# A hybrid decoder step on one core: eight weight slots in place of six, the cache copies at other tiles, weights laid out in long runs

## The chip, the cores and the metric

The kernel runs on one core of one Trainium2 chip. The metric is the device time of one execution in microseconds (us). Before the change, three runs gave a median of 1416.43 us (1415.73 to 1416.78).

## The reference, cut to what matters

One layer of a decoder, all in float32, for 256 prompt tokens and 8 sample tokens together (T = 264 columns, D = 1024):

```
h = rmsnorm(x); z = h @ w_in                      # 68 tiles of 128 columns: q, k, v, lru x, gates
b_lru = (rglru(conv(xr)) * gelu(gr)) @ w_br_lru    # recurrent branch
b_att = attention(q, k, v, caches) @ w_br_att      # 3 groups of dilated windows, 4 heads each
x = x + (sigmoid(g_lru)*b_lru + sigmoid(g_att)*b_att) @ w_out
x = x + moe(rmsnorm(x))                            # 32 experts, top 4, clamped SwiGLU
x = x + sigmoid(rmsnorm(x) @ w_ple_gate) * (p @ w_ple)
kv_g*_sample = cache shifted by one row, new k, v appended   # a copy of nearly the whole cache
```

Each expert has a 1024 x 2048 matrix (gate, up) and a 1024 x 1024 matrix (down): 12 MB, read once. The three sample caches (8 samples, windows of 128, 512 and 1024 rows of 4 KB) are copied to outputs with all rows one place down.

## The kernel before, in words

Five engines run their own instruction lists and meet at semaphores. SP issues nearly all loads, ACT (beside its activations) issues the cache copies, POOL issues small stores and the experts' biases. TensorE (PE) is the engine with the most work.

**Front.** The projection z runs in 68 tiles (`z_tile(n)`, L522 for its matmuls). Its weights come in 17 pieces of 2 MB (`win(piece)`, L393), four tiles each. Pieces 0 to 9 rotate through four ring slots, later ones through two; SP waits for `z_done` before it refills a slot: piece 9 when 24 tiles are done, piece 10 at 36, piece 11 at 40, piece 14 at 52. PE needs piece p at tile 4p. Between the tiles PE does other work in a written order: query and key norms after tile 25, the recurrent gates (L568) after tiles 41 to 44, transposes to token order (L554) after 45 to 50, prompt attention (L582, L594, L602) after 51 to 60, sample attention after 61 to 66. The transposes need `roped`, which VectorE (DVE) gives with L1255 after a small DMA of POOL has landed.

ACT evacuates each tile from PSUM (`evac`, L974) and between evacuations issues copies: `shift(g, b)` (L980) copies the cache of group g and sample b inside HBM, without its first row: 448 KB for group 0, 1984 KB for group 1, 4032 KB for group 2. The copies for groups 0 and 1 go out every fourth tile. Those of group 2 go out three together after tile 23, then after tiles 35, 43 and 51, and the last two (samples 6 and 7) when the first tile of the w_out product (L726) is done. The few rows that remain follow in `shift_rest`.

After the z tiles come the products with w_br_lru (L691), w_br_att (L701) and w_out (L726), whose halves SP loads (`half`, L433) with four runs of 4 KB for each partition; then the router and the PLE product p @ w_ple (L757).

**Experts.** The 32 experts run one after the other, each in six pieces of 2 MB: gate 0, gate 1, up 0, up 1, down 0, down 1. The ring has six slots, so piece s of expert e goes into the slot that piece s of expert e-1 leaves:

```python
for s in range(6):
    sp.wait_ge(used[s], n)
    sp.dma_start(slot(s), weights(e, s)).then_inc(full[s], 16)
```

SP issues the loads at L478. PE multiplies a piece with L789 (16 matmuls) and spreads the previous expert's rows to the tokens in between (L829). Expert 0's six pieces are loaded while the products ahead of the experts run. Experts 2 to 30 are one loop of PE, `pe.Fori(2, E - 1)`, with one expert in a pass. Code for the case that more than 64 tokens choose one expert (`further`) stands behind it and is jumped over when it isn't needed.

**Tail.** When gate 1 of expert 31 is done (`g1_mm`), SP loads the 4 MB of w_ple_gate into two slots. PE then does the PLE gate product (L937, L947), which waits for both halves, and the result is stored in four DMAs (L492). At the end SP waits for all stores and cache copies.

Of the kernel before, what the change touches and what calls it, by code (L numbers as in the profile page):

```python
# [14 lines left out]
P = 128  # L15
D = 1024
KT = D // P
NP, NS = 256, 8
T = NP + NS
# [6 lines left out]
DIL = (1, 4, 16)  # L26
SKEYS = tuple(w // d for w, d in zip(WB, DIL))
E = 32
# [5 lines left out]
CH = 512  # L34
# [27 lines left out]
class Signals:  # L62


    def __init__(self, sem):
# [76 lines left out]
        self.lru_x = sem("lru_x")  # L142
# [44 lines left out]
        self.bdn_in = sem("bdn_in")  # L187
# [16 lines left out]
        self.w5 = sem("w5")  # L204
        self.g0_mm = sem("g0_mm")
# [38 lines left out]
def build(nc, a):  # L244

    with ExitStack() as ctx:
        def sb(name, shape, dt=F32):
            return ctx.enter_context(nc.sbuf_tensor(name, shape, dt))
# [12 lines left out]
        hT = sb("hT", [P, KT, T])  # L261
        xc = sb("xc", [P, KT, T])
        lt = sb("lt", [P, KT, T])
# [28 lines left out]
        lt_flat = lt[:, :, :].rearrange("p k t -> p (k t)")  # L292
# [20 lines left out]
        wpl, pT = zb([P, 2, D]), zb([P, 2, T])  # L313
        wr = zb([P, KT, E])
# [16 lines left out]
        rparts = zb([P, T])  # L331
# [5 lines left out]
        wpg = [ring[:, SLOT[s], :].rearrange("p (k n) -> p k n", k=4) for s in (0, 1)]  # L337
# [6 lines left out]
        def further(eng, count, block_of, first, last, before=None, after=None):  # L344


            def chunk(c):
                if before is not None:
                    before(c)
                with eng.Fori(0, E) as e:  # L350
                    block_of(e, e + c * E)
# [32 lines left out]
        def _(sp):  # L384
# [42 lines left out]
            def cached_v(g, p0=0):  # L427
                n = SKEYS[g]
                src = a[f"cache{g}"].rearrange("b (k r) n -> k b r n", r=DIL[g])[:, :, 0, CH:2 * CH]
                sp.dma_start(vts[g][p0:p0 + n, :, :], src).then_inc(S.v_in, 16)  # L430
# [6 lines left out]
            cached_v(2, 64)  # L437
# [11 lines left out]
            sp.dma_start(wr[:, :, :], a["w_router"].rearrange("(k p) n -> p k n", p=P)).then_inc(S.wr_in, 16)  # L449
            sp.dma_start(wpl, a["w_ple"].rearrange("(k p) n -> p k n", p=P)).then_inc(S.wpl_in, 16)  # L450
            sp.dma_start(pT, a["pT"]).then_inc(S.wpl_in, 16)
            sp.dma_start(bdn, a["b_down"]).then_inc(S.bdn_in, 16)


            def weights(e, s):

                return a["wmoe"][e][s]

            def slot(s):
                return ring[:, SLOT[s], :]  # L460

            full = (S.w0, S.w1, S.w2, S.w3, S.w4, S.w5)
            used = (S.g0_mm, S.g1_mm, S.u0_mm, S.u1_mm, S.d0_mm, S.d1_mm)
            sp.dma_start(slot(0), weights(0, 0)).then_inc(S.w0, 16)
            sp.wait_ge(S.bl_mm, KT)
            sp.dma_start(slot(1), weights(0, 1)).then_inc(S.w1, 16)
            sp.dma_start(slot(2), weights(0, 2)).then_inc(S.w2, 16)
            sp.wait_ge(S.ba_mm, KT)
            sp.dma_start(slot(3), weights(0, 3)).then_inc(S.w3, 16)
            sp.wait_ge(S.wo_mm, KT)  # L470
            sp.dma_start(slot(4), weights(0, 4)).then_inc(S.w4, 16)
            sp.dma_start(slot(5), weights(0, 5)).then_inc(S.w5, 16)

            def load(e, n):

                for s in range(6):
                    sp.wait_ge(used[s], n)
                    sp.dma_start(slot(s), weights(e, s)).then_inc(full[s], 16)  # L478

            load(1, 1)  # L480
            count = load_most(sp)
            with sp.Fori(2, E) as e:
                load(e, e)
            further(sp, count, load, first=lambda: sp.wait_ge(S.d1_mm, E), last=lambda: sp.wait_ge(S.yb_zero, 1),
                    after=lambda n: sp.wait_ge(S.d1_mm, n))

            sp.wait_ge(S.g1_mm, E)
# [12 lines left out]
        def _(pe):  # L500
# [132 lines left out]
            def sample_attend():  # L633
                pe.wait_ge(S.st_ev, 3)
                pe.wait_ge(S.sb_ev, 1)
                pe.wait_ge(S.v_in, 64)
# [108 lines left out]
            pe.wait_ge(S.wpl_in, 32)  # L745
# [37 lines left out]
            def half_product(bank, src, slot):  # L783

                w = ring[:, SLOT[slot], :].rearrange("p (k n) -> p k n", k=4)
# [55 lines left out]
            def block_(n, following=True, alone=False):  # L841


# [6 lines left out]
                pe.wait_ge(S.w0, 16 * (n + 1))  # L850
                pe.wait_ge(S.xT_ok, n + 1)
                half_product(0, xgT, 0).then_inc(S.g0_mm, 1)
# [4 lines left out]
                pe.wait_ge(S.w1, 16 * (n + 1))  # L857
                half_product(0, xgT, 1).then_inc(S.g1_mm, 1)
                between(1)
                pe.wait_ge(S.w2, 16 * (n + 1))  # L860
                half_product(1, xgT, 2).then_inc(S.u0_mm, 1)
                between(2)
                pe.wait_ge(S.w3, 16 * (n + 1))
                half_product(1, xgT, 3).then_inc(S.u1_mm, 1)
# [11 lines left out]
                pe.wait_ge(S.w4, 16 * (n + 1))  # L876
                pe.wait_ge(S.hT_ok, n + 1)
                half_product(4, hmT, 4).then_inc(S.d0_mm, 1)
                pe.wait_ge(S.w5, 16 * (n + 1))
                half_product(4, hmT, 5).then_inc(S.d1_mm, 1)  # L880
# [22 lines left out]
            pe.wait_ge(S.bdn_in, 16)  # L903
            block_(0)
            block_(1)
# [5 lines left out]
            def apart(e, n):  # L911
                rows(n)
                rows_T(n)
                block_(n, following=False, alone=True)
                spread_all(n)

            further(pe, count, apart, first=lambda: spread_all(E - 1), last=lambda: pe.wait_ge(S.yb_zero, 1),
                    after=lambda n: pe.wait_ge(S.added, 4 * n + 4))
# [34 lines left out]
        def _(act):  # L953
# [69 lines left out]
            for n in range(24, NZ):  # L1023
# [7 lines left out]
                if n in (35, 43, 51):  # L1031
                    shift(2, n // 8 - 1)
# [54 lines left out]
            act.wait_ge(S.wo_mm, 1)  # L1087
            for b in range(6, NS):
                shift(2, b)
# [71 lines left out]

            root(3, rstd[:, :], PS[:, 0, 0:T], 1.0 / D).then_inc(S.rms_ok, 1)
# [6 lines left out]
        def _(v):  # L1169
# [92 lines left out]
            TT(X, X, xc[:, :, :], ALU.mult).then_inc(S.lru_x, 1)  # L1262
# [3 lines left out]
            v.wait_ge(S.lru_x, 1)  # L1266
# [358 lines left out]
def layout(i):  # L1625
# [5 lines left out]
    def cols(v):  # L1631
# [3 lines left out]

    order = [4, 5, 6, 7, 8, 9, 0, 1, 10, 11, 12, 2, 3, 13, 14, 15, 16]
# [10 lines left out]
        w_router=i["w_router"][0], b_router=np.ascontiguousarray(np.tile(i["b_router"], (P, 1))), w_br_lru=i["w_br_lru"][0], w_br_att=i["w_br_att"][0],  # L1647
        w_out=i["w_out"][0], w_ple_gate=i["w_ple_gate"][0],
        w_ple=i["w_ple"][0])
    for g in range(NG):  # L1650
        c = i[f"cache_kv_g{g}"][0]
        out[f"cache{g}"] = c.reshape(NS, WB[g], 2 * CH)
        out[f"kt{g}"] = np.ascontiguousarray(c[:, ::DIL[g], 0].transpose(3, 0, 2, 1)).reshape(P, -1)
# [54 lines left out]
```

## Time and profile before

| | |
|---|---|
| median of 3 runs | 1416.43 us |
| the profiled execution's own time | 1418.05 us |
| span of that execution | 1416.4 us |
| PE busy | 1350.0 us, 95% |
| DVE, ACT, POOL busy | 399.8, 182.4, 35.6 us |
| DMA moved | 531.41 MB, mean 375 GB/s |
| chain that ended last, by engine | PE 59%, DMA 39% |

The span runs from the first to the last instruction of the program. A number with L is a line of the kernel. A duration behind a DMA goes from its issue to its landing. "SPq" and "ACTq" are the instruction queues of SP and ACT, in which they wait and issue DMAs. q1 is the DMA queue that SP fills, q10 that of ACT, q0 that of POOL, q8 brings instructions.

### The profile page before, as it was taken

Reading aid. Unit: us, or ns where it says so; the run is one execution under the profiler, and the core shown is the slowest. Engines: PE = TensorE matmul, PEld = TensorE weight load, DVE = VectorE, ACT = ScalarE, POOL = GpSimd, SP = SyncE. Lnnn points to the kernel's source line nnn. Section 1 sums busy time; section 2 is a strip of 40 time slices with the busy share of each in tenths; the row PEclk is TensorE's granted clock in tenths of the full one; section 3 lists DMA queues with packets and bytes.
Section 4 is the critical chain, followed back from the end, with each engine's and each line's share of the span. In section 5 each row is a group of like instructions: output and inputs, shape, how many; then the busy total and the mean of one; then the engine's idle time right before and its main releaser. Section 6 shows DMA issues by size and latency. Waiting matters only on the chain.

```text
span 1416.4 us, 17044 instructions
## 1 busy us (share of the span) xinstructions
PE 1350.0 (95%) x7000; PEld 676.8 (48%) x7000; DVE 399.8 (28%) x636; ACT 182.4 (13%) x340; POOL 35.6 (3%) x62
## 2 busy tenths in 40 slices
PE   7999599899999999999999999999999999999988
PEld 6887488798874333333333333333333333333337
DVE  4106547320233222222222122221222212222134
ACT  1111034322003100010001000010000100000101
POOL 0001003000000000000000000000000000000000
PEclk9999899999999999999999999999999999999999
DMA  9889997958986999999999999999999999999980
GB/s 385 312 345 326 304 353 259 294 137 328 376 308 242 400 422 429 428 428 428 428 428 428 428 428 428 427 429 427 428 428 427 430 427 429 426 429 428 428 344 31
DMA packets 44886, 531.41 MB, mean 375 GB/s; under 512 B 6973, under 2 KB 7373, under 8 KB 16533
## 3 DMA queue, kind: packets, MB, share of 16 engines
q1 hardware_dynamic: 40784, 471.47, 80.9%
q10 hardware_dynamic: 1685, 54.43, 10.6%
q0 software_dynamic: 2384, 5.03, 1.2%
q8 instruction: 25, 0.41, 0.1%
q14 instruction: 8, 0.07, 0.0%
HBM read 526.15 MB, written 58.38 MB: 413 GB/s over the span
## 4 chain that ended last, share of the span: by engine, by line
PE 59%; DMA 39%; ACT 1%; DVE 0%; issue 0%; SPq 0%; DVEq 0%
DMA ring<-in_wmoe 33%; PE PS L789 25%; PE PS L522 16%; DMA ring<-in_win 5%; PE PS L829 2%; PE PS L726 2%; PE PS L691 2%; PE PS L803 2%; DMA ring<-in_w_ple_gate 2%; PE PS L937 1%; PE PS L947 1%; PE PS L701 1%; PE PS L568 1%; PE PS L815 1%; PE PS L795 1%; ACT Zb L1124 1%
## 5 line engine op out<-in xcount | busy, mean ns | idle before, releaser
L789 PE MATMUL PS<-ring,Zb 128*64 128x512 f32 x3072 | 687.6, 596 | 20.2 <-DMA ring<-in_wmoe 19.2
L789 PEld LDWEIGHTS PS<-ring,Zb 128*64 128x64 f32 x3072 | 209.4, 137 | 421.7 <-issue 378.7
L522 PE MATMUL PS<-hT,ring 128*128 128x264 f32 x1024 | 237.9, 392 | 21.8 <-DMA ring<-in_win 21.8
L522 PEld LDWEIGHTS PS<-hT,ring 128*128 128x128 f32 x1024 | 195.4, 193 | 58.5 <-DMA ring<-in_win 22.4
L1451 DVE TENSOR_TENSOR xc<-xc,PS 128x528 f32<-128x528 f32 x128 | 89.7, 701 | 171.8 <-PE PS L829 159.5
L1479 DVE COPY Zb<-PS 128x512 f32<-128x512 f32 x32 | 22.1, 692 | 326.7 <-PE PS L789 326.7
L829 PE MATMUL PS<-Zb 64*128 64x264 f32 x496 | 88.7, 435 | 0.0
L829 PEld LDWEIGHTS PS<-Zb 64*128 64x128 f32 x496 | 37.3, 184 | 100.6 <-issue 100.6
L1132 ACT ACTIVATE Zb<-Zb 128x512 f32<-128x512 f32 x32 | 20.2, 630 | 470.2 <-DVE Zb L1461 470.2
L1124 ACT ACTIVATE Zb<-PS 128x512 f32<-128x512 f32 x32 | 19.1, 597 | 358.0 <-PE PS L817 358.0
L803 PE MATMUL PS<-Zb 128*64 128x512 f32 x256 | 63.5, 617 | 0.0
L974 ACT ACTIVATE Zb<-PS 128x264 f32<-128x264 f32 (+1 forms) x64 | 25.0, 391 | 215.7 <-PE PS L522 215.7
L1470 DVE TENSOR_SCALAR Zb<-PS 128x512 f32<-128x512 f32 x32 | 22.1, 692 | 104.7 <-PE PS L789 104.7
L1461 DVE TENSOR_SCALAR Zb<-PS 128x512 f32<-128x512 f32 x32 | 22.1, 692 | 92.2 <-PE PS L789 92.2
L795 PE MATMUL PS<-cst,Zb 128*128 128x128 f32 x256 | 41.9, 286 | 6.4 <-ACT Zb L1124 5.5
L795 PEld LDWEIGHTS PS<-cst,Zb 128*128 128x128 f32 x256 | 26.8, 140 | 39.5 <-issue 25.3
L378 POOL DMA_DIRECT2D Zb<-in_b_gu x31 | 16.3, 527 | 918.1 <-PE PS L816 918.1
L817 PE MATMUL PS<-Zb 8*64 8x512 f32 x128 | 34.8, 613 | 0.0
L816 PE MATMUL PS<-Zb,cst 1*64 1x512 f32 x128 | 34.8, 613 | 0.0
L815 PE MATMUL PS<-Zb,cst 1*64 1x512 f32 x128 | 34.8, 613 | 0.0
L803 PEld LDWEIGHTS PS<-Zb 128*64 128x64 f32 x256 | 15.8, 138 | 30.2 <-issue 30.2
L726 PE MATMUL PS<-hT,ring 128*128 128x264 f32 x128 | 30.0, 390 | 0.0
(246 smaller groups left out, 844.6 us busy)
## 6 DMA issues: line engine op xcount, KB each, us to landing
ring<-in_wmoe SPq DMA_DIRECT2D x192, 2048.0 KB, 22.8
ring<-in_win SPq DMA_DIRECT2D x16, 2048.0 KB, 15.5
out_kvs<-in_cache ACTq DMA_DIRECT2D x8, 4032.0 KB, 28.9
out_kvs<-in_cache ACTq DMA_DIRECT2D x8, 1984.0 KB, 13.2
ring<-in_kt SPq DMA_DIRECT2D x2, 2048.0 KB, 24.5
ring<-in_cache SPq DMA_DIRECT2D x2, 2048.0 KB, 10.8
ring<-in_w_br_lru SPq DMA_DIRECT2D x2, 2048.0 KB, 17.9
ring<-in_w_out SPq DMA_DIRECT2D x2, 2048.0 KB, 19.6
```

The costliest lines, as they stand in the source:

```text
L522: last = mm(PS[:, bank, 0:T], w[:, k, :], (lt if piece == 0 else hT)[:, k, :], start=(k == 0), stop=(k == KT - 1))
L691: last = mm(PS[:, m % 4, 0:T], wbl[k // 4][:, k % 4, m * P:(m + 1) * P], Z[:, ZGR + k, :], start=(k == 0), stop=(k == KT - 1))
L726: last = mm(PS[:, 3 + m % 2, 0:T], wout[k // 4][:, k % 4, m * P:(m + 1) * P], hT[:, k, :], start=(k == 0), stop=(k == KT - 1))
L789: last = mm(PS[CAP * h:CAP * (h + 1), bank, :], src[:, k, f:f + CAP], w[:, k, h * CH:(h + 1) * CH], start=(slot == 4 and k == 0), stop=(sl ...
L795: last = nc.tensor.transpose(PS[:, bank, j * P:(j + 1) * P], src[:, j * P:(j + 1) * P], ident)
L803: mm(PS[CAP * h:CAP * (h + 1), 5, :], pick[:, b, :], hrow[:, b, h * CH:(h + 1) * CH], start=(b == 0), stop=False)
L815: mm(PS[half, 0, :], ones[0:1, 0:CAP], brow[0:1, cols], start=True, stop=False)
L816: seeded = mm(PS[half, 1, :], ones[32:33, 0:CAP], brow[32:33, cols], start=True, stop=False)
L817: last = mm(PS[half, 5, :], pick[ROWS[2], 2, :], hrow[ROWS[2], 2, cols], start=False, stop=True)
L829: last = mm(PS[:, 2 + h, 0:T], yb[CAP * h:CAP * (h + 1), j * P:(j + 1) * P], gpickT[CAP * h:CAP * (h + 1), :], start=True, stop=True)
L1124: A(xg, PS[:, 5, :], ACT.Copy).then_inc(S.xg_ok, 1)
L1451: TT(x, x, PS[:, 2:4, 0:T], ALU.add).then_inc(S.added, 1)
```

## The change

1. Two more 2 MB slots: one over `hT` and `lt` (now one tensor `hl`), one in a `zone` of scratch memory that also holds the router and PLE weights. Eight slots rotate: piece s of expert 4i+j goes into slot (6j+s) % 8. Pieces 0 and 1 of expert 1 are loaded ahead of the experts. Each later load waits for the piece eight places before it, where it waited for the one six places before it.
2. PE's expert loop has four experts in a pass: `pe.Fori(1, E // 4 - 1)`, six passes. SP's loop likewise.
3. The w_ple_gate load waits for `d1_mm >= E - 1` (expert 30 done) in place of `g1_mm >= E`, because expert 31 does not use slots 0 and 1.
4. The copies of group 2: sample 0 after tile 15, samples 1 to 4 after tiles 25, 38, 42 and 53, sample 5 when the second tile of the w_br_lru product is done, samples 6 and 7 when w_ple_gate has landed.
5. `w_br_lru`, `w_br_att`, `w_out`, `w_ple_gate`, `w_router`, `w_ple` and the sample's cached values come in layouts made on the host, so that a partition's data is one run. The values of group 2 come twice in one array and take one DMA instead of two.
6. The semaphores `lru_x` and `bdn_in` go: the first is a wait of DVE on its own instruction in place, the second counts on `wpl_in`. The load of b_down waits for `satt`.

```diff
+        hl = sb("hl", [P, 2 * KT * T])
...
+        zone = zb([P, 4096])
...
+        slots = [ring[:, s, :] for s in SLOT] + [hl[:, 0:4096], zone]
+        def place(j, s):
+            return (6 * j + s) % 8, (6 * j + s) // 8
...
             def half(w, k0, view, sem):
-                sp.dma_start(view, w[k0 * P:(k0 + 4) * P, :].rearrange("(k p) n -> p k n", p=P)).then_inc(sem, 16)
+                sp.dma_start(view, w[k0 // 4]).then_inc(sem, 16)
...
+            sp.wait_ge(S.ss_sum, 2)
+            sp.dma_start(slots[6], weights(1, 0)).then_inc(S.w6, 16)
+            sp.wait_ge(S.pl_mm, KT)
+            sp.dma_start(slots[7], weights(1, 1)).then_inc(S.w7, 16)
+            def load(e, j, n, pieces=range(6)):
+                for s in pieces:
+                    if s < 2:
+                        sp.wait_ge(used[s + 4], n - 1)
+                    else:
+                        sp.wait_ge(used[s - 2], n)
+                    at = place(j, s)[0]
+                    sp.dma_start(slots[at], weights(e, s)).then_inc(full[at], 16)
...
-            sp.wait_ge(S.g1_mm, E)
+            sp.wait_ge(S.d1_mm, E - 1)
             half(a["w_ple_gate"], 0, wpg[0], S.wpg_in)
...
+            def half_product(bank, src, slot, i, j):
+                at, fill = place(j, slot)
+                pe.wait_ge(full[at], 16 * (3 * i + fill + 1))
...
-            with pe.Fori(2, E - 1) as e:
-                block_(e)
-            block_(E - 1, following=False)
+            with pe.Fori(1, E // 4 - 1) as i:
+                for j in range(4):
+                    block_(i, j)
...
-            with act.Fori(1, 6) as i:
+            with act.Fori(1, 4) as i:
                 for t in range(4):
                     evac(4 * i + t, t)
                 shift(0, i)
                 shift(1, i)
-            for b in range(3):
-                shift(2, b)
+            shift(2, 0)
+            with act.Fori(4, 6) as i:
...
-                if n in (35, 43, 51):
-                    shift(2, n // 8 - 1)
+                if n in (25, 38, 42, 53):
+                    shift(2, (25, 38, 42, 53).index(n) + 1)
...
-            act.wait_ge(S.wo_mm, 1)
-            for b in range(6, NS):
-                shift(2, b)
+            act.wait_ge(S.bl_mm, 2)
+            shift(2, 5)
...
+            act.wait_ge(S.wpg_in, 32)
+            shift(2, 6)
+            shift(2, 7)
             root(3, rstd[:, :], PS[:, 0, 0:T], 1.0 / D).then_inc(S.rms_ok, 1)
```

## Rows read from the trace of the kernel before

**Rows 1.** The page's 40 slices: PE busy in tenths, GB/s.

```profile
PE   7999599899999999999999999999999999999988
...
GB/s 385 312 345 326 304 353 259 294 137 328 376 308 242 400 422 429 428 428 428 428 428 428 428 428 428 427 429 427 428 428 427 430 427 429 426 429 428 428 344 31
```

**Rows 2.** Busy time by stretch: start:end, length, engines, clock, DMA share, GB/s.

```profile
0.00:442.30 442.30, 409.76 (x2302) 340.77 (x2302) 160.82 (x249) 92.11 (x171) 19.76 (x32) 0.97 0.86 307
442.30:802.40 360.10, 357.95 (x1794) 122.44 (x1796) 85.83 (x139) 33.31 (x62) 6.31 (x12) 1.00 0.99 417
802.40:1352.20 549.80, 527.83 (x2663) 178.97 (x2659) 125.89 (x203) 49.09 (x94) 9.48 (x18) 1.00 1.01 428
...
1381.20:1416.40 35.20, 30.88 (x130) 25.75 (x130) 17.29 (x32) 5.06 (x10) 0.00 (x0) 0.95 0.08 31
```

**Rows 3.** Waits of PE, 0 to 440 us: total us, times, longest us.

```profile
PE PS L522 <- DMA ring<-in_win: 30.0, 3, 16.6
PE PS L772 <- DVE Zb L1398: 1.1, 1, 1.1
PE PS L594 <- DVE ring L1303: 1.1, 1, 1.1
```

**Rows 4.** Timeline of PE, two places: start us, us, instruction [idle before].

```profile
177.72 4.55 PE L522 MATMUL PS<-hT,ring 128*128 128x264 f32 x13 [16.61 <-DMA ring<-in_win]
...
274.14 6.49 PE L522 MATMUL PS<-hT,ring 128*128 128x264 f32 x16 [5.17 <-DMA ring<-in_win]
```

**Rows 5.** Chain that ended last, front: start us, us, what.

```profile
136.00 10.89 PE PS L522 x48
146.91 30.77 DMA ring<-in_win
...
214.98 1.31 PE PS L554 x12
...
244.25 29.85 DMA ring<-in_win
...
389.78 10.68 PE PS L726 x48
```

**Rows 6.** DMA issues at 68.4, 98 to 100, 146.9, 200.8, 244.2, 267.0 us.

```profile
ring<-in_win SPq DMA_DIRECT2D x1, 2048.0 KB, 13.9
...
out_kvs<-in_cache ACTq DMA_DIRECT2D x3, 4032.0 KB, 47.8
...
ring<-in_win SPq DMA_DIRECT2D x1, 2048.0 KB, 30.8
...
ring<-in_win SPq DMA_DIRECT2D x1, 2048.0 KB, 19.8
...
out_kvs<-in_cache ACTq DMA_DIRECT2D x1, 4032.0 KB, 30.0
ring<-in_win SPq DMA_DIRECT2D x1, 2048.0 KB, 29.9
...
ring<-in_win SPq DMA_DIRECT2D x1, 2048.0 KB, 19.1
```

**Rows 7.** DMA queues, 146.9 to 177.7 us: packets, MB, share of 16 engines.

```profile
q10 hardware_dynamic: 178, 6.62, 54.2%
q1 hardware_dynamic: 185, 2.51, 27.9%
q0 software_dynamic: 126, 0.90, 15.2%
```

**Rows 8.** Timeline of DVE around the rotary step.

```profile
187.19 6.75 DVE L1255 TENSOR_TENSOR Zb<-Zb,ring 32x6336 f32<-32x6336 f32 x1
```

**Rows 9.** DMA issues: w_out (345 to 349), one copy at 393.3, both at 393.9.

```profile
ring<-in_w_out SPq DMA_DIRECT2D x2, 2048.0 KB, 19.6
...
out_kvs<-in_cache ACTq DMA_DIRECT2D x1, 4032.0 KB, 17.2
...
out_kvs<-in_cache ACTq DMA_DIRECT2D x2, 4032.0 KB, 22.6
```

**Rows 10.** Chain that ended last, experts and tail.

```profile
442.33 3.65 PE PS L789 x16
...
465.75 10.45 PE PS L789 x48
...
494.23 10.45 PE PS L789 x48
...
802.35 25.08 DMA ring<-in_wmoe
...
831.34 25.77 DMA ring<-in_wmoe
...
1306.31 25.79 DMA ring<-in_wmoe
...
1341.13 10.45 PE PS L789 x48
...
1356.30 24.91 DMA ring<-in_w_ple_gate
1381.25 16.20 PE PS L937 x64
```

**Rows 11.** DMA 450 to 800 us: the instruction queue, issues and landings.

```profile
q8 instruction: 3, 0.05, 0.0%
...
ring<-in_wmoe SPq DMA_DIRECT2D x74, 2048.0 KB, 16.9
Zb<-in_b_gu POOLq DMA_DIRECT2D x12, 8.0 KB, 5.6
```

**Rows 12.** One expert load at 446.0, the loads of 800 to 1330 us.

```profile
ring<-in_wmoe SPq DMA_DIRECT2D x1, 2048.0 KB, 7.7
...
ring<-in_wmoe SPq DMA_DIRECT2D x107, 2048.0 KB, 25.0
```

**Rows 13.** The page's instruction queue: packets, MB, share.

```profile
q8 instruction: 25, 0.41, 0.1%
```

**Rows 14.** Timeline of the tail: the last stores.

```profile
1405.58 8.99 SPq L492 DMA_DIRECT2D out_yT<-Zb  x4
```

More of the change, by code:

```diff
@@ L204, in __init__ @@
         self.w5 = sem("w5")
+        self.w6 = sem("w6")
+        self.w7 = sem("w7")
         self.g0_mm = sem("g0_mm")
@@ L336, in build @@
         sgp = Z[:, 0:KT, :]
-        wpg = [ring[:, SLOT[s], :].rearrange("p (k n) -> p k n", k=4) for s in (0, 1)]
+        slots = [ring[:, s, :] for s in SLOT] + [hl[:, 0:4096], zone]
+        wpg = [slots[s].rearrange("p (k n) -> p k n", k=4) for s in (0, 1)]
+        def place(j, s):
+            return (6 * j + s) % 8, (6 * j + s) // 8
         def load_most(eng):
@@ L342, in load_most, with further @@
             return eng.value_load(most, min_val=0, max_val=T)
-        def further(eng, count, block_of, first, last, before=None, after=None):
+        def further(eng, count, block_of, first, last, before=None, after=None, fours=False):
             def chunk(c):
@@ L349, in chunk @@
                     before(c)
-                with eng.Fori(0, E) as e:
-                    block_of(e, e + c * E)
+                if fours:
+                    with eng.Fori(0, E // 4) as i:
+                        for j in range(4):
+                            block_of(i, j, i + c * (E // 4))
+                else:
+                    with eng.Fori(0, E) as e:
+                        block_of(e, e + c * E)
                 if after is not None:
@@ L455, in weights @@
+            sp.dma_start(bdn, a["b_down"]).then_inc(S.wpl_in, 16)
             def weights(e, s):
                 return a["wmoe"][e][s]
-            def slot(s):
-                return ring[:, SLOT[s], :]
-            full = (S.w0, S.w1, S.w2, S.w3, S.w4, S.w5)
+            full = (S.w0, S.w1, S.w2, S.w3, S.w4, S.w5, S.w6, S.w7)
             used = (S.g0_mm, S.g1_mm, S.u0_mm, S.u1_mm, S.d0_mm, S.d1_mm)
-            sp.dma_start(slot(0), weights(0, 0)).then_inc(S.w0, 16)
+            sp.dma_start(slots[0], weights(0, 0)).then_inc(S.w0, 16)
@@ L472, in _ @@
[L472 to L480, printed above, removed]
-            count = load_most(sp)
[L482 to L485, printed above, removed]
@@ L487, in _ @@
-            sp.wait_ge(S.g1_mm, E)
+            sp.dma_start(slots[4], weights(0, 4)).then_inc(S.w4, 16)
+            sp.dma_start(slots[5], weights(0, 5)).then_inc(S.w5, 16)
+            sp.wait_ge(S.ss_sum, 2)
[6 more added lines that the diff above has]
+                        sp.wait_ge(used[s + 4], n - 1)
+                    else:
+                        sp.wait_ge(used[s - 2], n)
+                    at = place(j, s)[0]
+                    sp.dma_start(slots[at], weights(e, s)).then_inc(full[at], 16)
@@ new lines, in _ @@
+            load(1, 1, 1, range(2, 6))
+            load(2, 2, 2)
+            load(3, 3, 3)
+            count = load_most(sp)
+            with sp.Fori(1, E // 4) as i:
+                for j in range(4):
+                    load(4 * i + j, j, 4 * i + j)
+            further(sp, count, lambda i, j, m: load(4 * i + j, j, 4 * m + j), first=lambda: sp.wait_ge(S.d1_mm, E),
+                    last=lambda: sp.wait_ge(S.yb_zero, 1), after=lambda n: sp.wait_ge(S.d1_mm, n), fours=True)
+            sp.wait_ge(S.d1_mm, E - 1)
@@ L778, in _ @@
             last.then_inc(S.rk_mm, 1)
-            def half_product(bank, src, slot):
-                w = ring[:, SLOT[slot], :].rearrange("p (k n) -> p k n", k=4)
+            full = (S.w0, S.w1, S.w2, S.w3, S.w4, S.w5, S.w6, S.w7)
+            def half_product(bank, src, slot, i, j):
+                at, fill = place(j, slot)
+                pe.wait_ge(full[at], 16 * (3 * i + fill + 1))
+                w = slots[at].rearrange("p (k n) -> p k n", k=4)
                 f = slot % 2 * CAP
@@ L839, in spread_bias, with block_ @@
                 last.then_inc(S.c_mm, 1)
-            def block_(n, following=True, alone=False):
+            def block_(i, jn, following=True, alone=False):
+                n = 4 * i + jn
                 def between(j):
@@ L902, in _, with apart @@
             pe.wait_ge(S.gT_ok, 1)
-            pe.wait_ge(S.bdn_in, 16)
-            block_(0)
-            block_(1)
+            for j in range(4):
+                block_(0, j)
             count = load_most(pe)
-            with pe.Fori(2, E - 1) as e:
-                block_(e)
-            block_(E - 1, following=False)
-            def apart(e, n):
+            with pe.Fori(1, E // 4 - 1) as i:
+                for j in range(4):
+                    block_(i, j)
+            for j in range(4):
+                block_(E // 4 - 1, j, following=(j < 3))
+            def apart(i, j, m):
+                n = 4 * m + j
                 rows(n)
                 rows_T(n)
-                block_(n, following=False, alone=True)
+                block_(m, j, following=False, alone=True)
                 spread_all(n)
             further(pe, count, apart, first=lambda: spread_all(E - 1), last=lambda: pe.wait_ge(S.yb_zero, 1),
-                    after=lambda n: pe.wait_ge(S.added, 4 * n + 4))
+                    after=lambda n: pe.wait_ge(S.added, 4 * n + 4), fours=True)
             pe.wait_ge(S.added, 4 * E)
@@ L995, in _ @@
                 shift(1, i)
-            for b in range(3):
-                shift(2, b)
+            shift(2, 0)
+            with act.Fori(4, 6) as i:
+                for t in range(4):
+                    evac(4 * i + t, t)
+                shift(0, i)
+                shift(1, i)
             def gate_out(i):
```

72 lines of the change are left out of this document (33 added, 39 removed).

## The prediction

> **What bounds the kernel now.** I read the slices first, then the busy times by stretch, the waits of PE, and the chain in order of time. The slices show PE in its highest tenth nearly everywhere, with gaps in the first, fifth and eighth slice [rows 1]. By stretch there are three regimes [rows 2]. Up to 442.3 us PE is busy for 409.8 us at 307 GB/s: the DMAs are not full on average. From there to 1352 us the DMA share is 0.99 and then 1.01, at 417 and 428 GB/s: the experts' weights fill the queue. In the last 35.2 us nothing but the tail of PE runs, at 31 GB/s.
>
> In the front PE waits for hardly anything but projection weights: three waits, 30.0 us in all [rows 3]. Two are in the timeline, 16.61 us ahead of tile 40 and 5.17 us ahead of tile 56 [rows 4]; the third, 8.2 us, is the first load of all, which nothing in the change touches.
>
> In the experts the chain goes through PE up to 802 us and through the weight loads from there [rows 10]. That looks like two bounds, but it is one. PE alone needs 494.23 - 465.75 = 28.48 us for an expert. The loads need (1306.31 - 831.34) / 16 = 29.69 us, 4.95 for each of the six. PE starts with a lead of six loaded pieces and loses 1.2 us of it per expert, until a load is late at 802 us. The loads were the slower side from the start: one issued at 446.0 lands after 7.7 us, the median up to 800 us is 16.9 and after it 25.0, so the queue only gets longer [rows 11, 12].
>
> **The change part by part.**
>
> *Copies at other tiles.* Piece 10 is issued at 146.91 and lands after 30.8 us [rows 5, 6], because three copies of 4 MB were issued together at 98 us and their median landing is 47.8 us, so one is still whole then. A fourth is issued at the same moment as piece 10. While PE waits, the copies' queue takes 54.2% of the engines' time and SP's 27.9% [rows 7]. After the change the first of the three goes at tile 15, the second at tile 25, and the third at tile 38, three tiles (10.9 us [rows 5]) after piece 10; the fourth comes later still. Piece 10 then has small copies beside it at most, as the piece issued at 68.4 us had, which took 13.9 us [rows 6]: it would land at 160.8. It is needed at 177.72 - 16.61 = 161.1. I take the stall as gone, 16.6 us. Bounds: with a whole copy beside it, 19.8 us as at 200.8 [rows 6], a stall of 5.6 stays; at worst all 16.6 stays; below nothing can't come here, since the pieces that the moved copies now meet (7 to 9) are refilled 12 tiles or some 43 us ahead of their use, more than the 30.8 us of the worst such load.
>
> Piece 14 is issued at 244.25 beside the sixth copy and lands after 29.9 us, 5.17 too late [rows 4, 6]; it had 24.7 us. Now the fifth copy goes two tiles (over 7 us) later and the sixth not here. The load at 267.0, beside other loads and the end of a copy, took 19.1 us [rows 6]. I take 5.2 us; bounds 0 and 5.2.
>
> What is late next: PE comes to the transposes (L554) at 214.98 - 16.6 = 198.4. They need DVE's L1255, which ended at 193.94 [rows 5, 8]; a cover of 4.4 us, and the small DMA that DVE waited for has fewer copies beside it now. The sixth copy moves in among the loads of w_out, which land some 20 us after 347 and are needed at 389.78 [rows 5, 9]. 4.13 MB at that slice's 376 GB/s [rows 1] delays them by 11 us to about 381: hidden, with 9 us to spare; without that cover it would cost its excess one for one.
>
> *Two more slots.* PE's start of the experts sets when slots come free. Between 425 and 446 us the queue runs dry (242 GB/s in that slice [rows 1], and the landing of 7.7 us). The two added loads fall in there: one at the router's sums, about 424, one at the last PLE product, about 441, landing by 449. Each load from 446 on is therefore two places further in the same stream: 2 x 4.95 = 9.9 us at its end. Bounds: 0 if they only take the place of others; 21.0 at most, because with PE alone expert 30's down product would start at 465.75 + 30 x 28.48 = 1320.1 in place of 1341.13 [rows 10]. So the loads still end last, by 11.1 us, and I take 9.9.
>
> *The PLE gate's weights.* They are issued at 1355.85 and land at 1381.21 [rows 10], two loads of 4.95 behind the last expert load: the queue sets that, not the issue. Issued earlier they stand at the same place in the stream, 9.9 us earlier with it. PE's last spreads are done 1.2 us before that landing, so an even earlier one would bring no more than 1.2.
>
> *Two copies in the tail.* After the landing there are 35.2 us [rows 2]. The pair at 393 us landed after 17.2 and 2 x 22.6 - 17.2 = 28.0 us, with a weight load beside it [rows 9]. With 0.6 us between the issues that is 28.6, and ends 6.6 us before the end. The stores start at 1405.58, 24.4 us after the landing [rows 14]: some 4 us of overlap, not with the last store. Cost 0; bounds 0 and, at the 30.0 us of the slowest lone copy [rows 6], 2 x 30.0 - 35.2 = 24.8. Taking them out from 393 us gains nothing by itself: the loads behind them wait for the w_out product anyway.
>
> *Layouts, semaphores.* None of the loads that get long runs ends a wait of PE [rows 3], so faster landings are worth 0, and so is SP's shorter issue; the cover is that PE is behind them all. DVE's wait on its own instruction stands between two instructions that DVE does in order anyway.
>
> *Four experts in a pass.* The instructions are the same ones. What may cost is the way back to the loop's start. From 802.4 to 1352.2 us PE does 2663 matmuls [rows 2], so 2663 x 29.69 / 549.8 = 144 for an expert, with a weight load each: 288 instructions, 1150 in a pass. The instruction queue brings 0.41 / 25 = 16 KB at a time, and only three times between 450 and 800 us [rows 11, 13]: the present loop stays where it is. No row shows a loop four times as long. I take 0; bounds 0 and, per way back, the 5.6 us in which an 8 KB load lands in the full queue [rows 11], the nearest small transfer. Six passes go back five times: 28.0 us, of which PE has the 11.1 in hand: 16.9.
>
> The Trainium skill speaks on this, in "Runtime: NRT & Kernel Launch", section "Instruction fetch mechanics": instructions come in 16 KB blocks of 256, and a taken branch to a target outside the present two-block window stalls until the block is fetched; for PE it also gives a store of 128 KB, or 2048 instructions. By the first a pass of 1150 stalls on every way back, by the second it does not. The trace agrees on the block's size; that the loop of one expert runs without fetches fits both.
>
> *Sum.* 16.6 + 5.2 + 9.9 = 31.7 us. The profiled execution's span is 1416.4, its own time 1418.05, the median of the runs 1416.43; the span stands for the median. 1416.4 - 31.7 = 1384.7 us.
>
> **The rivals.**
>
> A. The front keeps a part of its stalls: a copy still stands beside piece 10, or DVE's cover of 4.4 us is used up. For it: copies take twice the time of loads when they meet [rows 7], and the third goes out before piece 10 has surely landed. Against it: 10.9 us ahead of that copy. It gives 1384.7 + 5.6 = 1390 up to 1406.5, if all 21.8 stay.
>
> B. The way back of PE's loop stalls, and this one can end slower than before. Its place is the five ways back of the pass of four. At 5.6 us each it gives 1384.7 + 16.9 = 1402. It breaks even with before at (31.7 + 11.1) / 5 = 8.6 us each. Should the fetch wait as long as a weight load does late in the stream, 25.0 us [rows 12], it would be 5 x 25.0 - 11.1 = 113.9 on top: 1499. Against it: three fetches came through the full queue while PE kept its 28.48 us.
>
> C. The copies in the tail end last: up to 1384.7 + 24.8 = 1409.5. For it: lone copies of 30.0 us [rows 6]. Against it: those had loads and small stores beside them, and the tail has a DMA share of 0.08 [rows 2].
>
> D. The slots don't give a longer lead, because the two loads merely push the next ones: 1384.7 + 9.9 = 1394.6. Against it: the dry queue before 446 us.
>
> E. The stream also loses less than I think, and PE alone bounds: 1384.7 - 11.1 = 1373.6. Against it: 428 GB/s in every slice leaves nothing to win [rows 1].
>
> **How the numbers follow.** Forecast 0.66, A 0.14, B 0.09 (0.04 of it slower), C 0.05, D 0.03, E 0.03. The forecast's own range is 1378 to 1391: a few us for margins of 0.3 and 4 us in the front. For 8 in 10 it goes down to 1376, and up to 1403, through most of A, all of D and the mild form of B. About 0.2%, 2.8 us, is what a measurement of this kernel tells from no change. Slower: 0.04 from B and 0.01 from C. Same: 0.01 from B and 0.01 from C. Faster: 0.93.
>
> **What would show it.** Right: PE's waits for projection weights fall from 30.0 to about 8 us; the experts begin (first L789) near 420.5 instead of 442.33; the chain turns from PE to loads some eight experts later (9.9 / 1.2) than the twelfth; the PLE gate's weights land near 1349.5; 35 us follow them, and both copies land before the last store. Wrong: a wait ahead of tile 40 of over 5 us, or of PE for DVE there (A); idle PE at every fourth expert, and fetches in the experts' stretch (B); the chain ending in a copy (C); loads that turn late at the twelfth expert again (D).

## The result, and the profile after

The kernel as changed takes 1403.7 us (median of 6, 1401.45 to 1408.49) against 1416.61 for the one before on the same chip: ratio 0.9904, 95% interval 0.9886 to 0.9922. The forecast was 1384.7, so less than half of the 31.7 us came. The profiled execution has a span of 1403.1 (own time 1404.75), 13.3 less than before.

The page of after, its 40 slices: PE busy in tenths and GB/s, beside [rows 1].

```profile
PE   7999679999999999999999999999999999999988
...
GB/s 383 318 347 368 253 209 263 243 230 308 384 204 347 401 424 427 427 427 427 427 428 427 429 427 429 427 428 428 427 428 428 428 427 428 428 428 427 428 370 267
```

PE still has its hole in the fifth slice, now running into the sixth, while the DMAs move 253 and 209 GB/s, against some 428 among the experts. The hole of the eighth slice is closed.

Busy time by stretch in after, cut at its own stages (columns as in [rows 2]): up to the first expert, expert products until loads are late, those after, and the tail.

```profile
0.00:440.50 440.50, 406.07 (x2302) 338.85 (x2302) 162.38 (x249) 92.13 (x171) 19.74 (x32) 0.98 0.82 294
440.50:1000.00 559.50, 556.11 (x2797) 189.96 (x2797) 133.66 (x216) 51.62 (x97) 9.97 (x19) 1.00 1.00 424
1000.00:1352.00 352.00, 339.01 (x1710) 114.96 (x1708) 81.40 (x131) 31.41 (x60) 5.77 (x11) 1.00 1.01 428
1369.60:1403.10 33.50, 29.22 (x132) 24.62 (x130) 18.41 (x34) 6.35 (x11) 0.00 (x0) 1.00 0.84 279
```

The chain that ended last in after, experts and tail, beside [rows 10].

```profile
440.52 3.65 PE PS L812 x16
...
463.95 10.45 PE PS L812 x48
...
492.42 10.45 PE PS L812 x48
...
577.86 10.45 PE PS L812 x48
...
1005.02 10.45 PE PS L812 x48
...
1019.88 33.81 DMA ring<-in_wmoe
...
1369.64 14.50 PE PS L957 x64
```

Three differences make up the 13.3 us. The first expert starts at 440.52 in place of 442.33: 1.8. From there to the PLE gate's product it is 929.1 in place of 1381.25 - 442.33 = 938.9: 9.8. From that product to the end 33.5 in place of 35.2: 1.7, all in the first block of that product (14.50 in place of 16.20), whose granted clock was 0.61 over the first 3.75 us in before and is 1.00 now. So the slots brought what was forecast, and the front brought 1.8 in place of 21.8.

The waits and the timeline of PE in after, front, beside [rows 3, 4].

```profile
PE PS L541 <- DMA ring<-in_win: 31.7, 3, 22.6
```

```profile
148.21 14.51 PE L541 MATMUL PS<-hl,ring 128*128 128x264 f32 x64 [0.90 <-DMA ring<-in_win]
185.27 8.81 PE L541 MATMUL PS<-hl,ring 128*128 128x264 f32 x32 [22.55 <-DMA ring<-in_win]
```

The wait at tile 56 is gone, the one at tile 40 has grown from 16.61 to 22.55, and tile 36 waits 0.9 for piece 9. The loads of SP show why. DMA issues of after at 69.2, 83, 97, 114.6, 147.3 and 159.2 us (KB, us to landing), which answer to [rows 6].

```profile
brt<-in_b_router SPq DMA_DIRECT2D x1, 16.0 KB, 31.6
...
ring<-in_win SPq DMA_DIRECT2D x1, 2048.0 KB, 38.5
...
ring<-in_win SPq DMA_DIRECT2D x1, 2048.0 KB, 50.8
...
ring<-in_wrg SPq DMA_DIRECT2D x1, 2048.0 KB, 56.3
...
ring<-in_win SPq DMA_DIRECT2D x1, 2048.0 KB, 37.9
...
out_kvs<-in_cache ACTq DMA_DIRECT2D x1, 4032.0 KB, 23.7
```

These stand in one queue. The bias of the router, 128 rows of 128 bytes, takes 31.6 us; piece 8 behind it 38.5; piece 9 behind that 50.8; the gates' weights, issued at 114.56, 56.3. They land at 170.89, and piece 10, issued at 147.34, after them at 185.23. What one packet waits for is seen in the queues of after from 82 to 90 us: packets, MB, share of 16 engines (q1 is SP's, q10 ACT's).

```profile
q10 hardware_dynamic: 32, 2.06, 81.0%
q1 hardware_dynamic: 32, 0.00, 0.3%
```

As many packets from SP as from ACT; but ACT's are pieces of a cache copy (2.06 MB / 32 = 64 kB each), and SP's are bias rows. Each row of 128 bytes waited for a copy's packet. The Trainium skill says that an SDMA engine takes turns between its queue rows packet by packet ("DMA: Bandwidth & Descriptors", section "Queues, rings and completion order"); 32 to 32 at 2.06 MB to almost none agrees with it.

Later, from the issue of piece 10 to its landing, the queues of after from 147.3 to 185.2 us (q0 is POOL's), beside [rows 7]:

```profile
q1 hardware_dynamic: 346, 5.14, 48.4%
q10 hardware_dynamic: 113, 5.21, 34.8%
q0 software_dynamic: 118, 0.88, 15.3%
```

The copy, the rest of the gates' weights and piece 10 share those engines with POOL's stores. The shares add up to 98.5%: the engines are busy nearly all the time, though they move only 11.23 MB in 37.9 us, 296 GB/s. The packets take longer.

In the tail and around it (DMA issues at 1337 and 1369.6 us, then the last stores on SP's timeline, beside [rows 14]):

```profile
ring<-in_w_ple_gate SPq DMA_DIRECT2D x2, 2048.0 KB, 28.4
...
out_kvs<-in_cache ACTq DMA_DIRECT2D x2, 4032.0 KB, 22.2
...
1392.27 9.00 SPq L511 DMA_DIRECT2D out_yT<-Zb  x4
```

The gate's weights landed at 1369.58, PE was there at 1369.64. The copies landed at 1385.44 and 1398.76, 4.3 us ahead of the end.

### The profile page after: what moved, and what is told of

Read it like the earlier page. It is cut to its first block, busy times and chain, and to the rows that moved or that the text cites. A ratio compares the mean times of both kernels' runs of the same rounds, so it can differ in the third digit from the quotient of the medians.

```text
span 1403.1 us, 16858 instructions
## 1 busy us (share of the span) xinstructions
PE 1343.5 (96%) x7000; PEld 673.4 (48%) x7000; DVE 401.3 (29%) x636; ACT 182.4 (13%) x340; POOL 35.5 (3%) x62
## 4 chain that ended last, share of the span: by engine, by line
PE 78%; DMA 18%; ACT 2%; DVE 1%; issue 0%; SPq 0%; DVEq 0%
PE PS L812 38%; PE PS L541 16%; DMA ring<-in_wmoe 15%; PE PS L852 4%; PE PS L826 3%; DMA ring<-in_win 3%; PE PS L745 2%; PE PS L710 2%; PE PS L838 2%; PE PS L818 1%; ACT Zb L1147 1%; PE PS L957 1%; PE PS L967 1%; PE PS L720 1%; PE PS L587 1%; PE PS L894 1%
## 5 line engine op out<-in xcount | busy, mean ns | idle before, releaser
L812 PE MATMUL PS<-ring,Zb 128*64 128x512 f32 x2304 | 517.0, 596 | 8.2 <-DMA ring<-in_wmoe 7.5
L812 PEld LDWEIGHTS PS<-ring,Zb 128*64 128x64 f32 x2304 | 156.8, 137 | 308.6 <-issue 290.4
L541 PE MATMUL PS<-hl,ring 128*128 128x264 f32 x1088 | 252.8, 392 | 31.7 <-DMA ring<-in_win 31.7
L541 PEld LDWEIGHTS PS<-hl,ring 128*128 128x128 f32 x1088 | 207.5, 193 | 70.7 <-DMA ring<-in_win 32.6
L812 PE MATMUL PS<-Zb 128*64 128x512 f32 x384 | 87.3, 596 | 1.8 <-DMA Zb<-in_wmoe 1.8
L812 PE MATMUL PS<-hl,Zb 128*64 128x512 f32 x384 | 87.3, 596 | 1.7 <-DMA hl<-in_wmoe 1.4
L826 PE MATMUL PS<-Zb 128*64 128x512 f32 x256 | 62.0, 605 | 0.0
L812 PEld LDWEIGHTS PS<-Zb 128*64 128x64 f32 x384 | 26.1, 137 | 53.2 <-issue 48.9
L812 PEld LDWEIGHTS PS<-hl,Zb 128*64 128x64 f32 x384 | 26.2, 137 | 50.6 <-issue 47.4
L818 PEld LDWEIGHTS PS<-cst,Zb 128*128 128x128 f32 x256 | 26.9, 140 | 39.5 <-issue 25.3
```

The costliest lines, as they stand in the source:

```text
L541: last = mm(PS[:, bank, 0:T], w[:, k, :], (lt if piece == 0 else hT)[:, k, :], start=(k == 0), stop=(k == KT - 1))
L818: last = nc.tensor.transpose(PS[:, bank, j * P:(j + 1) * P], src[:, j * P:(j + 1) * P], ident)
L826: mm(PS[CAP * h:CAP * (h + 1), 5, :], pick[:, b, :], hrow[:, b, h * CH:(h + 1) * CH], start=(b == 0), stop=False)
```

## The experiments

The theories as the first expectations number them. 1: the bias rows, put beside the first copy by the change, hold up SP's queue. 2: the copies of tiles 15 and 25 do, as such. 3: the third copy, at tile 38, takes the engines from piece 10. From the fifth run on, P: POOL's stores of the conv states (by the program runs of 12, 64 and 32 bytes) slow every packet; Q: the copies of tiles 15 and 25 hold up SP's queue (theory 2 again). Ratios are to the kernel before, each on its own chip with its own runs of it.

**e1_bias_early.** The bias is loaded at the start, behind `gqk`.

```
+            sp.dma_start(brt[:, :], a["b_router"]).then_inc(S.wr_in, 16)
...
-                if piece == 7:
-                    sp.dma_start(brt[:, :], a["b_router"]).then_inc(S.wr_in, 16)
```

> The changed kernel with one load moved: the router bias (128 rows of 128 bytes, behind piece 7 at 69 us in the changed kernel) is issued among the first loads. Theory 1, small rows: in the queue that SP fills, each row of 128 bytes takes a turn against a whole 64.5 KB packet of the copy issued at 70.6 us, so pieces 8, 9, the gate weights and piece 10 start some 16 us late; without it piece 8 lands before 112 us instead of 121.6, the stall ahead of tile 40 falls from 22.6 to under 8 us, and the time to 1384 to 1391. Theory 2, copies as such: the 4 MB copies of tiles 15 and 25 take the queue's share, the bias is a bystander; the stall stays over 18 us and the time within 3 us of 1403.7. Theory 3, the third copy: the copy at tile 38 holds piece 10; as theory 2.

Ratio 0.9903 (0.9883 to 0.9923), span 1396.7. Piece 8 landed at 106.05 in place of 121.61 and the gates' weights at 155.24 in place of 170.89, as theory 1 had it; but piece 10 landed at 178.88, with the third copy at 178.68, and the wait at tile 40 was 19.4. The bias rows' delay was gone and most of the stall was not: theory 1 alone falls.

**e2_copy_late.** The third and fourth copy after tiles 42 and 48.

```
-                if n in (25, 38, 42, 53):
+                if n in (25, 42, 48, 53):
```

> The changed kernel with the copies of samples 2 and 3 after tiles 42 and 48 instead of 38 and 42; the bias stays behind piece 7. Theory 1: the queue ahead of piece 10 ends only when the gate weights land near 171 us; piece 10 then lands near 177, the stall ahead of tile 40 is 12 to 16 us instead of 22.6, the time 1394 to 1398. Theory 2: the stall falls by no more than 4 us. Theory 3: the stall falls under 5 us and the time to 1384 to 1388.

Ratio 0.9841 (0.982 to 0.9862), wait at tile 40 9.5, between what theories 1 and 3 gave (12 to 16, under 5); theory 2, which allowed 4 us less than 22.6, falls as the only cause. The gates' weights still landed late, at 164.45.

**e3_both.** The edits of e1 and e2.

> Both edits: the bias among the first loads, and samples 2 and 3 after tiles 42 and 48. Theory 1: nothing is left ahead of tile 40, stall under 2 us, time 1380 to 1386, near the predicted 1384.7. Theory 2: a stall of 10 us or more stays from the copies of tiles 15 and 25. Theory 3: as in the run with the copy late alone, no better.

Ratio 0.9834 (0.9806 to 0.9863), span 1384.6. No 4 MB copy stood beside piece 10 any more and SP's queue had lost the bias rows, yet PE waited 6.1, which none of the three theories had given:

```profile
166.16 8.92 PE L540 MATMUL PS<-hl,ring 128*128 128x264 f32 x32 [6.12 <-DMA ring<-in_win]
```

**e4_slots_alone.** All copies at their old places, none in the tail; the slots, the pass of four and the layouts as changed.

```
+            with act.Fori(1, 6) as i:
...
+            for b in range(3):
+                shift(2, b)
...
+                if n in (35, 43, 51):
+                    shift(2, n // 8 - 1)
...
+            act.wait_ge(S.wo_mm, 1)
+            for b in range(6, NS):
+                shift(2, b)
...
-            act.wait_ge(S.wpg_in, 32)
-            shift(2, 6)
-            shift(2, 7)
```

> The changed kernel with all copies at the places of the kernel before (three after tile 23, then 35, 43, 51, two when the w_out product starts): eight slots, the pass of four and the layouts alone. All theories on the front: stalls of 16.6 and 5.2 us as before, and the slots' term alone, 9.9 us: 1405 to 1408. If the slots' gain hung on the copies' places, it would be over 1411.

Ratio 0.9934 (0.9911 to 0.9957), median 1404.5, just under what was expected, span 1403.0. Its waits, timeline of PE:

```profile
177.11 9.09 PE L541 MATMUL PS<-hl,ring 128*128 128x264 f32 x32 [18.33 <-DMA ring<-in_win]
...
273.70 6.71 PE L541 MATMUL PS<-hl,ring 128*128 128x264 f32 x16 [5.04 <-DMA ring<-in_win]
```

Both stalls of before are back; the first expert starts at 440.46 and the PLE gate's product at 1369.65, 929.2 later. The slots, with the pass of four and the layouts, give the 9.7; where the change put the copies gave nothing more, and the two copies of the tail cost nothing (its tail is as long without them: 1403.0 - 1369.65 = 33.4).

**e5_no_conv.** e3_both without the three stores of the conv states; those two outputs stay unwritten.

```
-            po.dma_start(a["convp"], Z[:, ZX:ZX + KT, NP - 3:NP]).then_inc(S.conv_out, 16)
-            po.dma_start(a["convs"][:, :, 0:2 * NS], ...).then_inc(S.conv_out, 16)
-            po.dma_start(a["convs"][:, :, 2 * NS:3 * NS], Z[:, ZX:ZX + KT, NP:T]).then_inc(S.conv_out, 16)
```

> e3_both with the three stores of the conv states (POOL, 12, 64 and 32 KB in runs of 12 to 128 bytes) left out; both conv outputs are not written. Of the 7.1 us that PE still waits at tile 40 in e3_both: Theory P (POOL's tiny stores between 130 and 159 us slow every packet on the engines): piece 10, issued near 146, lands before 161 in place of 166.11, the wait falls under 2 us, the span goes from 1384.6 to some 1378 to 1380. Theory Q (the copies issued at tiles 15 and 25 hold up SP's loads ahead of piece 10: piece 9 took 32.8 us and the gates' weights 40.5): nothing of that changes, the gates' weights land near 153 and the wait stays at 6 to 8 us, the span at 1383 to 1386.

Ratio 0.9769 (0.9728 to 0.981), span 1375.2, no wait at tile 40. Piece 10 took 11.6 us in place of 20.3, the gates' weights landed at 147.07. With the 108 KB of stores PE's 6 us were gone. (The 7.1 us of the expectation are the first load's wait in e3_both; at tile 40 it was 6.12.)

**e6_second_45.** e3_both with the second copy at tile 45.

```
-                if n in (25, 42, 48, 53):
+                if n in (42, 45, 48, 53):
```

> e3_both with the second 4 MB copy at tile 45 in place of tile 25 (42, 45, 48, 53). Theory Q: without it piece 9 lands before 122 us (128.56) and the gates' weights before 146 (153.50), piece 10 before 160, the wait at tile 40 is under 1.5 us and the span near 1378. Theory P: the tiny stores come at the same times, so the wait keeps 5 us or more and the span 1382 to 1385. Against both: the moved copy meets the pieces for tiles 44 to 56 and makes a new wait there of a few us; then the sum of the waits for projection weights, 13.2 in e3_both, doesn't fall by as much as the wait at tile 40.

Ratio 0.9819 (0.9797 to 0.9841). Without that copy the gates' weights landed at 126.53, piece 10 at 158.45, and the wait at tile 40 went too, as theory Q had it, though the stores' runs were as short as before. But the copies now stood closer together later on. PE waited 3.87 us for the weights of tile 52, the new wait that the expectation set against both, and 2.13 us for DVE, which waited for POOL's stores of keys and values. First PE's timeline, then the chain:

```profile
228.19 5.51 PE L540 MATMUL PS<-hl,ring 128*128 128x264 f32 x16 [3.87 <-DMA ring<-in_win]
235.84 2.93 PE L600 MATMUL PS<-Zb 128*128 128x256 f32 x6 [2.13 <-DVE ring L1318]
```

```profile
207.54 1.03 POOL out_kvs L1593 x2
208.57 26.63 DMA out_kvs<-ring
```

**e7_packed.** e6_second_45 with the conv states packed by POOL before they are stored; each partition is then one run (96 and 768 bytes).

```
+            nc.gpsimd.tensor_copy(cvp[:, :, :], Z[:, ZX:ZX + KT, NP - 3:NP]).then_inc(S.q_zero, 1)
...
+            po.wait_ge(S.q_zero, 3)
+            po.dma_start(a["convp"], cvp[:, :, :]).then_inc(S.conv_out, 16)
+            po.dma_start(a["convs"], cvs[:, :, :]).then_inc(S.conv_out, 16)
```

> e6_second_45 with the conv states packed first: POOL copies them into a buffer of their own, so that each partition is stored in one run (96 bytes and 1.5 KB) and nothing waits for the stores any more. Theory P: what e6_second_45 still waits at tile 40 goes, the span is 1377 to 1379. Theory Q: no difference to e6_second_45 beyond 1 us. The best by either theory: 1379 to 1383 us as a median, below e3_both's 1389.5.

Ratio 0.9801 (0.978 to 0.9822). Tile 40 had no wait to lose, so the run tells nothing between P and Q; the waits at tile 52 (5.25) and for POOL's stores (28.1 us to landing) stayed. It does not reach the 1379 to 1383 of its expectation.

**e8_packed_e3.** The edits of e1, e2 and e7 together: e3_both with the packing.

> e3_both (bias load early, copies at 25, 42, 48, 53) with the conv states packed by POOL into a buffer of their own before they are stored, the whole result computed. Theory P (the tiny stores were what was left): piece 10, issued near 146, lands by 160, no wait at tile 40, PE's waits for projection weights are the first load's 5 to 6 us alone; span 1376 to 1379, median 1377 to 1383. Theory Q' (e5_no_conv was better because 108 KB of stores and the wait behind them were gone, not because of their run length): the wait at tile 40 stays above 3 us, span 1381 to 1385. The rest of the gain over the kernel as changed comes by the same step in both: no other wait of PE in the front.

1379.43 us, ratio 0.9751 (0.9728 to 0.9774), span 1377.7. The waits of PE in the front, and the queues from 130 to 160 us, first of e3_both, then of e8_packed_e3:

```profile
PE PS L541 <- DMA ring<-in_win: 7.0, 1, 7.0
```

```profile
q1 hardware_dynamic: 166, 2.46, 43.2%
q10 hardware_dynamic: 123, 4.08, 39.7%
q0 software_dynamic: 148, 0.90, 16.6%
```

```profile
q1 hardware_dynamic: 251, 3.59, 33.6%
q10 hardware_dynamic: 115, 3.63, 29.9%
q0 software_dynamic: 144, 0.92, 16.4%
```

The one wait left is the first load. POOL moves as many bytes in both, but a packet of SP's takes 0.432 x 480 / 166 = 1.25 us beside the short runs and 0.336 x 480 / 251 = 0.64 beside the packed ones (16 engines x 30 us = 480; means over the stretch). The cost lies in the packets of others, not in the stores' own time. So P holds, and Q' (the bytes and not the run length) falls.

**e9_after_packed.** The kernel as changed with the packing of e7 alone.

> The kernel as changed (copies at 25, 38, 42, 53, bias load late) with nothing but the conv states packed. It tells how the causes add. If the tiny stores alone make the packets slow and the copy at tile 38 only shares the engines: piece 10 lands about 37.9 - 6 to 10 us after its issue and the wait at tile 40 falls from 22.6 to 12 to 16 us. If the stores are the main cause whatever copy stands beside: below 5 us, median 1383 to 1388. If they matter only when nothing else is late: 20 us or more, 1401 to 1404.

Ratio 0.9862 (0.9838 to 0.9887). The profiled execution waited 7.5 us, but at 1387.66 it is the fastest by 6 us; the median of 1395.93 stands for a wait that was not seen. None of the three cases of the expectation fits both.

**e10_before_packed.** The kernel before with the packing alone.

> The kernel before, with nothing but the conv states packed before they are stored: it tells whether the tiny stores were already a cause of the 16.61 us at tile 40 that the prediction put down to three copies alone. If the copies alone set it: 15 to 17 us, 1412 to 1416. If the tiny stores take their part there as in e9_after_packed: 5 to 12 us, median 1404 to 1410, PE's waits for projection weights 18 to 25 us in place of 30.0; the wait at tile 56 (5.17 us) stays in both, since the sixth copy still stands beside piece 14.

Ratio 0.9954 (0.9935 to 0.9974), wait at tile 40 11.8 in place of 16.61, at tile 56 4.55. The median was 1410.82 against 1416.79, a little less than expected. The stores took part in the stall of before, which the prediction gave to copies alone.

**e11_packed_late, e12_packed_bias.** e8_packed_e3 with one of its other two edits taken back: the bias load late again (e11: the edits of e2 and e7), the copies at 25, 38, 42, 53 again (e12: those of e1 and e7).

> e8_packed_e3 with the bias load back at its late place (69 us, beside the first 4 MB copy). If the 128-byte rows hold up SP's queue for as long as in the kernel as changed (piece 8 lands near 119 us in place of 104.78, the gates' weights some 8 us later than 148.33, piece 10 near 164): a wait of 1 to 5 us at tile 40, median 1381 to 1385. If they no longer matter once the stores are packed and the third copy is late: no wait, median as e8_packed_e3 within 2 us (1377.5 to 1381.5).

> e8_packed_e3 with the copies back at 25, 38, 42, 53 (the third at tile 38, some 11 us after piece 10's issue). If a copy that goes out beside piece 10 costs by itself: piece 10, issued near 145, is still in flight when the copy starts near 156, a wait of 2 to 8 us, median 1383 to 1390. If the copy only costs where SP's queue is late: piece 10 lands near 157, as in e8_packed_e3, before the copy has moved anything; no wait at tile 40, median within 2 us of e8_packed_e3.

e11: ratio 0.9769 (0.9755 to 0.9784), piece 8 at 119.98, the gates' weights at 159.13, piece 10 at 164.01, a wait of 3.0. e12: 1379.09 us, ratio 0.9748 (0.9735 to 0.9762), no wait at tile 40, with the third copy where the change put it. Timeline of PE in e12, where after had its 22.55:

```profile
139.72 27.31 PE L541 MATMUL PS<-hl,ring 128*128 128x264 f32 x122
166.87 3.72 PE L587 MATMUL PS<-xc,ring 128*128 128x264 f32 x16
```

Piece 10 landed at 156.90 there, when the third copy, issued at 156.40, had moved next to nothing. The eight kernels together (ratio to before):

| | copies at 25, 38, 42, 53 | at 25, 42, 48, 53 |
|---|---|---|
| as changed | 0.9904 | 0.9841 (e2) |
| bias early | 0.9903 (e1) | 0.9834 (e3) |
| packed | 0.9862 (e9) | 0.9769 (e11) |
| bias early and packed | **0.9748 (e12)** | 0.9751 (e8) |

Read together, the wait at tile 40 takes two things at once. The short rows make SP's queue late where 4 MB copies stand beside them: the bias load took 13.9 us in the kernel before, with no 4 MB copy in flight, and e6 lost the wait with the stores unpacked, once the copy of tile 25 was gone. With long rows the copies cost nothing there: in e12 all of them are where the change has them, and no weights are late, so theories 2 and 3 hold only with the rows as they were. The third copy only makes a late piece later. The bias, which e1 showed to be worth nothing, is worth 0.9862 to 0.9748 once the stores are packed and the third copy stands at tile 38; with the copies late it is 0.9769 to 0.9751, within the intervals. That the stores' run length slows the other queues' packets is shown; by what mechanism inside the DMA engines is not.

## Why the prediction was wrong

The step that failed is the landing of piece 10: "Piece 10 then has small copies beside it at most", "it would land at 160.8", "I take the stall as gone, 16.6 us". It landed at 185.23, and the term measured -5.9; PE's waits for projection weights, which were to fall from 30.0 to about 8 us, rose to 31.7. Three things were left out of it.

- The loads ahead of it. The step looked at what stands beside piece 10, and not at what stands before it in SP's queue; and even beside it, by its own numbers, the third copy goes out 10.9 us after a load that takes 13.9. The gates' weights were in no sentence; they were 24 us from landing when piece 10 was issued. The sentence that excluded a loss ("the pieces that the moved copies now meet (7 to 9) are refilled 12 tiles or some 43 us ahead of their use, more than the 30.8 us of the worst such load") took a load's time in the old company for its worst: piece 9 took 50.8 and was late itself. The gates' weights had taken 39.5 us before the change already, with an issue at 114 and a landing at 153.6.
- The bias rows. The copy moved to tile 15 is issued 1.4 us after a load of 128 rows that took 13.9 us before and 31.6 now. e1 brings piece 8 back to 106.
- The conv stores, named nowhere: 108 KB looked like nothing, and were a part of the stall of before too (e10).

Rival A was thus what happened, with a price of 21.8 - 1.8 = 20.0, near its upper end; but neither of its two reasons is enough by itself (e12). Its "the third goes out before piece 10 has surely landed" is what makes the delay large, not what makes it. That it came out near A's end by these causes is chance.

What held:

- The term of 5.2 us at tile 56: the wait is gone in after. Its 16 matmuls also fell from 6.33 to 3.56 us, from their start to the next one's; they no longer follow an idle PE. Over 274.14 to 280.63 us of before the granted clock was 0.58, a mean between the levels of 1.2 and 2.4 GHz and mostly at the lower, after PE had stood still for 5.17 us; it was 1.00 in the stretch after.
- The slots' 9.9 us: 9.8 in after, 9.7 in e4. The chain turns to loads 1019.88 - 440.52 = 579.4 us into the experts in place of 360.0: 7.7 experts of 28.48 later, forecast eight. By the landings that PE waited for, 1053.69 and 827.43, it is 8.0.
- The pass of four, at nothing: from expert 4, the loop's first, to expert 19 one takes (1005.02 - 577.86) / 15 = 28.48 us, as before, with three ways back among them. The instruction queue brought 34 blocks in place of 25 [rows 13], and none between 655.9 and 1260.2 us, while PE went back from pass to pass. Rival B is out. Of the two rules that the Trainium skill gives in "Runtime: NRT & Kernel Launch", section "Instruction fetch mechanics", the trace agrees with the store of 128 KB, and shows no stall at the ways back.
- The copies of the tail, at nothing: 28.6 us forecast from the first issue to the last landing, 29.1 measured. Rival C is out; the PLE gate's weights and the layouts cost nothing either. The copy that moved in among the loads of w_out made PE wait for none of them.
- D and E are out by the same rows: the lead grew by the full 9.8, and a load still ends the last wait among the experts, at 1350.12. At the PLE gate PE came just as the weights landed (1369.64 and 1369.58), so the 1.2 us that it had waited there were gone.

Where the stalls do go (e12, e8) the kernel is some 5 us below the forecast. The forecast counted the waits alone; e8's first expert starts at 412.63 in place of the 420.5 that was expected. Of these 7.9, the first load is 1.2 shorter, which is luck: its wait lies between 6.5 and 8.3 in the runs here. From start to the next start, the 32 matmuls behind tile 40 take 7.12 in place of 8.62, those of tile 56 3.56 in place of 6.33, and the 8 that gather the first expert's rows (L826, before L803) 1.87 in place of 3.34. Those last three are clock, 5.7 in all: granted 0.83, 0.57 and 0.55 before, 1.00 in e8. The first two went with the waits. The third did not: it is 1.87 in after and e4 too, where the stall at tile 40 stayed. What raised the clock there stays open.

One more size stays open: what PE waits at tile 40 in an ordinary execution of e9, whose profile fell on its fastest.

## What to carry to other kernels

For a load that must land in time, list what stands before it in its own queue, back to the first load that can be late, and only then what stands beside it. Look at the length of a transfer's rows and not at its bytes: here 16 KB in rows of 128 bytes, beside a large copy, held up the 2 MB loads behind them, and 108 KB in runs of 12 to 64 bytes held up loads on another queue. When an experiment with one edit shows nothing, try it again on top of the others before the cause is dropped; here it took two repairs together to bring a ratio of 0.9748.

## What the runs showed of the hardware

A load of 16 KB in 128-byte rows took 31.6 us beside a 4 MB copy in packets of 64 kB, against 13.9 in the kernel before, with only smaller copies in flight. 108 KB of stores in runs of 12 to 64 bytes doubled the mean time of SP's packets (1.25 against 0.64 us). The Trainium skill puts the price of small descriptors on their own packets ("DMA: Bandwidth & Descriptors", section "Why small descriptors are slow (HBM only)"); here POOL's own packets took the same share either way (16.6% and 16.4%), and the price was seen in SP's. A wait of PE can also cost clock: after 22.55 us of it the next 8.8 us ran at a granted 0.83 (a third of them at 1.2 GHz, the rest at 2.4), and 32 matmuls took 8.65 us in place of 7.12.
